# A gated recurrence, latent attention and FFN on one core: the first product behind each norm multiplies scaled inputs, and root and shift enter behind it

## The reference

```python
def rms_norm_2(x, gain=None):
    y = xf * lax.rsqrt(jnp.mean(xf * xf, axis=-1, keepdims=True) + EPS)
...
    mod = (c @ w_ada + b_ada)[:, None, :]
    sh_m, sc_m, g_m, sh_f, sc_f, g_f = jnp.split(mod, 6, axis=-1)
    h = rms_norm_2(x) * (1 + sc_m) + sh_m
    proj = h @ w_in
    x_lru, q_down, kv_down, k_rope, gate_a, gate_b = jnp.split(proj, IN_SPLIT_POINTS, axis=-1)
    y_a = rg_lru(causal_depthwise_conv(x_lru, conv_w, conv_b), ...)
    y_b = mla(q_down, kv_down, k_rope, cos, sin, q_norm_g, kv_norm_g, w_uq, w_ukv)
    y = jax.nn.sigmoid(gate_a) * y_a + jax.nn.sigmoid(gate_b) * y_b
    x = x + g_m * (y @ w_out)
    h = rms_norm_2(x) * (1 + sc_f) + sh_f
    gate, up = jnp.split(h @ w_ffn_in, 2, axis=-1)
    x = x + g_f * ((jax.nn.silu(gate) * up) @ w_ffn_out)
```

## Time and profile before

| | us |
|---|---|
| median of 3 runs | 1828.05 (1827.4 to 1828.36) |
| the profiled execution | 1825.89 |
| its span, first to last instruction | 1824.1 |
| PE busy | 1751.8 (96%) |
| DVE busy | 956.1 (52%) |
| ACT busy | 723.8 (40%) |
| POOL busy | 688.3 (38%) |

### The profile page before, as it was taken

One profiled execution on the slowest core, in us unless ns is written; L12 is line 12 of the kernel. 1 busy time (PEld: TensorE's weight loads), 2 busy tenths in 40 slices (PEclk: granted clock), 3 DMA queues, 4 the chain that ended last, 5 costly groups with the idle time before them and its releaser, 6 DMA issues. The chain is left out here.

```text
span 1824.1 us, 23408 instructions
## 1 busy us (share of the span) xinstructions
PE 1751.8 (96%) x8349; PEld 1416.4 (78%) x8349; DVE 956.1 (52%) x1746; ACT 723.8 (40%) x1244; POOL 688.3 (38%) x303
## 2 busy tenths in 40 slices
PE   7999999988999999999999999999999999999997
PEld 6777777777888766788888887888766788888886
DVE  5999688584679577633343322579665311101112
ACT  5433655523375553322222222466553333222221
POOL 3424111236430334555445554440212454444442
PEclk9999999999999999999999999999999999999998
DMA  6234010053332224455555542233211232232211
GB/s 246 81 104 139 24 32 28 24 196 128 104 104 93 81 81 140 136 194 189 194 187 185 187 148 81 87 110 104 93 35 35 69 108 100 81 115 93 93 58 47
DMA packets 56634, 197.67 MB, mean 108 GB/s; under 512 B 6993, under 2 KB 8017, under 8 KB 56530
## 3 DMA queue, kind: packets, MB, share of 16 engines
q1 hardware_dynamic: 55666, 194.15, 31.6%
q10 hardware_dynamic: 864, 2.11, 0.3%
HBM read 194.14 MB, written 2.10 MB: 108 GB/s over the span
## 5 line engine op out<-in xcount | busy, mean ns | idle before, releaser
L491 POOL TENSOR_TENSOR WL<-RAW,WH 128x1024 fp32r<-128x1024 f32 x234 | 592.5, 2537 | 900.6 <-ACT WH L580 561.8
L1743 PE MATMUL bank<-HH,WH 128*128 128x512 f32 x1120 | 437.0, 390 | 7.8 <-POOLq L496 5.9
L1745 PE MATMUL bank<-HH,WL 128*128 128x512 f32 x1120 | 435.9, 389 | 0.0
L1744 PE MATMUL bank<-HL,WH 128*128 128x512 f32 x1120 | 435.8, 389 | 0.0
L580 ACT ACTIVATE WH<-RAW 128x1024 fp32r<-128x1024 f32 x259 | 270.6, 1051 | 243.8 <-PE bank L1745 218.1
L1743 PEld LDWEIGHTS bank<-HH,WH 128*128 128x128 f32 x1120 | 210.2, 188 | 53.3 <-issue 10.2
L1745 PEld LDWEIGHTS bank<-HH,WL 128*128 128x128 f32 x1120 | 210.2, 188 | 44.0
L1744 PEld LDWEIGHTS bank<-HL,WH 128*128 128x128 f32 x1120 | 210.2, 188 | 43.4
L1676 DVE TENSOR_TENSOR HF<-SILU,bank 128x512 f32<-128x512 f32 x44 | 30.3, 688 | 314.3 <-PE bank L1745 311.3
L1743 PE MATMUL bank<-HDH,WH 128*128 128x512 f32 x352 | 137.1, 389 | 0.0
L1745 PE MATMUL bank<-HDH,WL 128*128 128x512 f32 x352 | 136.9, 389 | 0.0
(11 more groups left out here) (363 smaller groups left out, 2839.6 us busy)
## 6 DMA issues: line engine op xcount, KB each, us to landing
RAW<-in_stream SPq DMA_DIRECT2D x363, 512.0 KB, 3.3
out_t<-YA SPq DMA_DIRECT2D x8, 256.0 KB, 2.2
X<-in_xt ACTq DMA_DIRECT2D x3, 512.0 KB, 11.3
RAW<-in_stream SPq DMA_DIRECT2D x2, 256.0 KB, 4.0
X<-in_xt ACTq DMA_DIRECT2D x2, 256.0 KB, 6.4
ACC<-in_pos SPq DMA_DIRECT2D x1, 256.0 KB
gains<-in_gains SPq DMA_DIRECT2D x1, 224.0 KB
CS<-in_cs SPq DMA_DIRECT2D x1, 128.0 KB
```

Of the source, the lines that this page charges most:

```text
L491: nc.gpsimd.tensor_tensor(lo(k)[:], raw(k)[:], hi(k)[:].bitcast(F32), ALU.subtract).then_inc(sem["passed"], mark("passed", *k))
L1743: nc.tensor.matmul(out, A[0], B[0], start=first, stop=False)
L1744: nc.tensor.matmul(out, A[0], B[1], start=False, stop=False)
L1745: return nc.tensor.matmul(out, A[1], B[0], start=False, stop=last)
```

## The change

The first product behind each norm (`kvq`; `fg` and `fu` tile 0) multiplies u = X(1 + scale), split into `plain_hi` on ACT and `plain_lo` on DVE: in `YH`, `YL` at m0, in `HH`, `HL` elsewhere. The root multiplies its result at the eviction. The shift's part of the product is a sum over raw weight rows times shift (`shift_times`, DVE, in `SHA`, made beside `o1`, `o2` and `fo`), which PE adds up over the partitions (`shift_sum`, `shift_columns`); it enters at the eviction too. PE takes the square sum behind `kvq` slot 0 (behind chunk 5 of `fg`), root and shift product behind slot 1 (behind chunk 3 of `fu`). POOL adds all eight squares, the warm matmuls are gone, and h is made as before, for the products that follow. Sixteen `ada` slots instead of eight are summed in the attention, eight instead of sixteen beside `o1`; the scale block of the mixer is turned in the attention.

```diff
-        order += [ada.pop(0) for _ in range((2, 3, 3, 3, 3, 2, 0, 0)[n])]
+        order += [ada.pop(0) for _ in range((2, 2, 2, 2, 0, 0, 0, 0)[n])]
...
-                order += [ada.pop(0) for _ in range((0, 1, 2, 2, 2, 1, 0, 0)[n])]
+                order += [ada.pop(0) for _ in range((1, 2, 2, 2, 1, 0, 0, 0)[n])]
...
-                    if ada:
+                    if ada and f:
...
-ATT_ADA = tuple(range(4, 76, 9))
+ATT_ADA = tuple(range(4, 84, 5))
...
-    return key[:2] == ("ada", 0) and key[2] // 8 in (0, MLA_CB)
+    return key[:2] == ("ada", 0) and key[2] // 8 in (0, 1, MLA_CB)
...
+def shift_product(key):
+    return key[0] == "kvq" or (key[0] in ("fg", "fu") and key[2] == 0)
...
+                        if shift_product(k):
+                            pool.wait_ge(sem["shift_mul"], value("shift_mul", *k))
...
-                for k in range(1, KD - 1):
+                for k in range(1, KD - (tag == "fin")):
...
+            def plain_hi(tag, k):
+                layer, cb = int(tag[1]), 1 if tag[0] == "m" else 4
+                act.wait_ge(sem["x_new"], value("x_new", tag, k))
+                act.wait_ge(step, value("scale", layer, cb))
+                nc.scalar.activation(plain(tag)[0][:, k, :], X[:, k, :], ACT.Identity,
+                                     scale=scale_of(tag)[:, k:k + 1]).then_inc(
+                    sem["u_hi"], mark("u_hi", tag, k))
...
+                    if tag == "m1":
+                        act.wait_ge(*last_use(("kvq", 1, k // 2)))
+                    elif tag[0] == "f" and k < KD - 1:
+                        act.wait_ge(sem["u_used"], value("u_used", tag, k))
+                    elif tag[0] == "f":
+                        act.wait_ge(*last_use(("fu", int(tag[1]), 0)))
...
+                    if tag[0] == "m" and k in (2, 4, 6):
+                        split_through(("kvq", int(tag[1]), k // 2))
...
-                act.wait_ge(sem["x_new"], value("x_new", "m0", n))
+                plain_hi("m0", n)
...
-                split_through(("kvq", L, 0), 0)
+                split_through(("kvq", L, 3), 0)
...
-                for tt in range(NT):
-                    evict(KVR[:, tt, :], "kvq", L, tt)
+                evict(SPREAD[:, 0:448], "shift", L)
...
+                    if L or n >= 5:
+                        for k in range(KD) if (L, n) == (0, 5) else (n,):
+                            if k <= n:
+                                plain_hi(f"f{L}", k)
...
+                split_through(("fg", L, 0))
...
+                evict(SPREAD[:], "rb", f"f{L}")
...
-                        evict(SILU[:, f % 2, :], "fg", L, f, func=ACT.Silu)
+                        if f:
+                            evict(SILU[:, f % 2, :], "fg", L, f, func=ACT.Silu)
+                        else:
+                            act.wait_ge(sem["scaled"], value("scaled", "fg", L))
+                            nc.scalar.activation(SILU[:, 0, :], NTMP[:, 0, :], ACT.Silu, bias=SHF[:, 0:1]).then_inc(
+                                sem["read_act"], mark("read_act", "fg", L, 0))
...
+                            if tag == "m1":
+                                plain_hi(tag, n)
...
+                        note[("scale", layer, cb)] = count["step"]
+            def plain_lo(tag, k):
+                dve.wait_ge(sem["u_hi"], value("u_hi", tag, k))
+                hi_, lo_ = plain(tag)
+                V.scalar_tensor_tensor(out=lo_[:, k, :], in0=X[:, k, :], scalar=scale_of(tag)[:, k:k + 1],
+                                       in1=hi_[:, k, :].bitcast(F32), op0=ALU.mult, op1=ALU.subtract).then_inc(
+                    sem["u_lo"], mark("u_lo", tag, k))
+            def shift_times(slot, shift, parts, dst):
+                dve.wait_ge(landed[ring(slot)], loads(slot))
+                for i, (k, col) in enumerate(parts):
+                    n = dst.shape[1]
+                    src = raw(slot)[:, col:col + n]
+                    if k == 0:
+                        ins = V.tensor_scalar(dst, src, shift[:, 0:1], None, ALU.mult)
+                    else:
+                        ins = V.scalar_tensor_tensor(out=dst, in0=src, scalar=shift[:, k:k + 1], in1=dst,
+                                                     op0=ALU.mult, op1=ALU.add)
+                    if i < len(parts) - 1:
+                        ins.then_inc(step, 1)
+                        dve.wait_ge(step, own())
+                ins.then_inc(sem["shift_mul"], mark("shift_mul", *slot))
+                dve.wait_ge(sem["shift_mul"], value("shift_mul", *slot))
+            def shift_rows(layer, s):
+                shift_times(("kvq", layer, s), mod[:, layer, 0:KD], [(2 * s + c, 512 * c) for c in range(2)],
+                            SHA[:, 0:448])
+            def shift_tile(layer, i):
+                shift_times((("fg", "fu")[i], layer, 0), mod[:, layer, 3 * KD:4 * KD],
+                            [(k, P * k) for k in range(KD)], SHA[:, i * P:(i + 1) * P])
...
-                mods(("o1", n)) if n < KD - 1 else None
-            ada_through(("xl", 0, 0))
-            mods(("o1", KD - 1))
+                mods(("o1", n))
+                if n:
+                    plain_lo("m0", n - 1)
+                if 3 <= n < KD - 1:
+                    shift_rows(0, n - 3)
+            plain_lo("m0", KD - 1)
...
-                dve.wait_ge(sem["read_act"], value("read_act", "kvq", L, NT - 1))
+                dve.wait_ge(sem["read_act"], value("read_act", "shift", L))
+                for t in range(NT):
+                    dve.wait_ge(sem["full"], value("full", "kvq", L, t))
+                    V.scalar_tensor_tensor(out=KVR[:, t, :], in0=bank_of("kvq", L, t)[:, 0:448],
+                                           scalar=stat[:, 1, t:t + 1], in1=SPREAD[:, 0:448],
+                                           op0=ALU.mult, op1=ALU.add).then_inc(
+                        sem["read_dve"], mark("read_dve", "kvq", L, t))
+                dve.wait_ge(sem["read_dve"], value("read_dve", "kvq", L, NT - 1))
...
+                    if n in (3, 4):
+                        shift_tile(L, n - 3)
+                    if L == 0 and n == 5:
+                        for k in range(n):
+                            plain_lo(f"f{L}", k)
+                    elif n and (L or n > 5):
+                        plain_lo(f"f{L}", n - 1)
+                plain_lo(f"f{L}", KD - 1)
...
+                        if f == 0:
+                            dve.wait_ge(sem["full"], value("full", "shift_f", L))
+                            b = bank_of("shift_f", L)
+                            V.tensor_copy(SHF[:], b[:, 0:2]).then_inc(sem["read_dve"], mark("read_dve", "shift_f", L))
+                            dve.wait_ge(sem["read_dve"], value("read_dve", "shift_f", L))
+                            dve.wait_ge(sem["read_act"], value("read_act", "rb", f"f{L}"))
+                            for i, kind in enumerate(("fg", "fu")):
+                                dve.wait_ge(sem["full"], value("full", kind, L, 0))
+                                V.tensor_tensor(NTMP[:, i, :], bank_of(kind, L, 0)[:], SPREAD[:],
+                                                ALU.mult).then_inc(sem["scaled"], mark("scaled", kind, L))
...
-                        dve.wait_ge(sem["full"], value("full", "fu", L, f))
-                        b = bank_of("fu", L, f)
-                        V.tensor_tensor(HF[:, f % 2, :], SILU[:, f % 2, :], b[:], ALU.mult).then_inc(
-                            sem["hid"], mark("hid", L, f))
+                        if f == 0:
+                            dve.wait_ge(sem["scaled"], value("scaled", "fu", L))
+                            V.scalar_tensor_tensor(out=HF[:, 0, :], in0=NTMP[:, 1, :], scalar=SHF[:, 1:2],
+                                                   in1=SILU[:, 0, :], op0=ALU.add, op1=ALU.mult).then_inc(
+                                sem["hid"], mark("hid", L, 0))
+                        else:
+                            dve.wait_ge(sem["full"], value("full", "fu", L, f))
+                            b = bank_of("fu", L, f)
+                            V.tensor_tensor(HF[:, f % 2, :], SILU[:, f % 2, :], b[:], ALU.mult).then_inc(
+                                sem["hid"], mark("hid", L, f))
...
+                        if half and L + 1 < LAYERS:
+                            if n:
+                                plain_lo(next_norm(L), n - 1)
+                            if n == KD - 1:
+                                plain_lo(next_norm(L), n)
+                            if 3 <= n < KD - 1:
+                                shift_rows(L + 1, n - 3)
...
-                pe.wait_ge(sem[adder], value(adder, tag, KD - 2))
+                pe.wait_ge(sem[adder], value(adder, tag, KD - 1 if newest is None else KD - 2))
...
-                warm(tag, 0, 7)
+            def root_rows(tag):
...
-                warm(tag, 1, 6)
...
+            def shift_sum(layer):
+                b = claim("shift", layer)
```

(23 more changed lines are left out.)

84 lines of the change are left out of this document (55 added, 29 removed).

## The result

The changed kernel takes 1845.84 us (median of four runs, 1843.0 to 1848.88) against 1828.2 of the kernel before beside it: ratio 1.0093, 95% interval 1.0073 to 1.0112. It is slower, by 17.6 us and not by the 8 of the forecast. The profiled execution took 1845.64 us, 19.75 more than the one before.

A forecast was written before the change was run, and what follows sets the result against it. TensorE, busy 1751.8 of 1824.1 us, was taken as the bound, with DVE-POOL blocking second. Against the profiled 1825.89: +1.4 - 5.1 + 1.4 + 2.5 - 4.2 - 4.4 = 8.4 slower, 1834.3, median 1836; own range 1830 to 1841, wide 1811 to 1846.

The forecast's parts named there:

- clock term: Half-clock falls after new PE stalls, charged for two at 2.2 us each: 4.4 us slower, bounds 0 and 10.8.
- The attention: Eight more slots scaled on ACT and added on POOL make PE wait: loss 4.2 us, bounds 1.5 and 6.
- Attention output and first mixer: Output stage through first mixer: square sum stalls 3.7 us, second XCL feeds PE at 480.5 against 481.96, gain 1.4.
- The unblocked T + 48.2 of the mixer: Second layer's mixer: second XCL ready at T + 48.2, T the sum's place, without DVE-POOL blocking; gain 5.0 us.
- First FFN: First FFN norm: late scale block stalls the square sum 4.2 us, third hidden tile starts late; loss 5.1 us.
- Second mixer: Second layer's mixer: second XCL ready at T + 51.8 against T + 53.2, T the sum's place; gain 1.4 us.
- Second FFN: Second FFN norm: scale ready early, sum waits about 0.1 us, third tile starts at 27.5; gain 2.5 us.
- two longest only: Choice to charge a clock fall only at the two longest of four new stalls: 2 x 2.2 = 4.4 us.
- All four stalls that I had listed: New PE stalls above 2.8 us: 3.7, 4.2, 6.7 at the third hidden tile, 3.1 at lg0.
- The rule: DVE-POOL port lock: by it HL, YL and the latents block beside POOL, giving the sum of 8.4 us slower.
- the covers hold: Rival: DVE-POOL blocking is rare, no stall long enough for the clock; 10.7 us faster, 1817; chance 0.34.
- a fall at every long stall: Rival: each of the four long stalls drops the clock; 14.8 us slower, 1843; chance 0.08.

The follow-up runs named there:

- e6: Changed kernel with one DVE step per shift product instead of two or eight, most of the shift's part left out of four products: 1832.83 us, ratio 1.0029.
- e1: Changed kernel with matmuls of no use put on TensorE ahead of nine waits: 1836.05 us, ratio 1.0044.
- e11: Changed kernel with one step for each shift product and matmuls of no use ahead of the waits: 1829.26 us, ratio 1.0005.
- e2: Kernel before with only the new plan of w_ada slots up to the attention output, no norm changed: 1831.52 us, ratio 1.0023.
- e4: Changed kernel with the first FFN's scaled inputs using the mixer's long-ready scale block, made chunk by chunk: 1844.27 us, ratio 1.0092.
- e9: Kernel before with only the second layer's two norms changed, plus matmuls of no use ahead of waits there and around the attention: 1824.76 us, ratio 0.9988.
- e7: Kernel before without its 52 warm matmuls at the four norms, nothing else changed: 1836.22 us, ratio 1.0048.

## Why the prediction was wrong

The direction was right, and the mechanism that I named, blocking between DVE and POOL together with the clock, is what the trace shows. The size was half of it: 8 us against 17.6. The wide range ended at 1846 and takes the result in by 0.2 us, which is luck; the forecast's own ended at 1841.

Two steps of the sum failed. The shift steps beside the FFN's output tiles had no term at all, and the clock was charged 4.4 us where 16.2 more of lost work came. They overlap: e6 is 13 us better without the steps, e1 9.8 with fills, e11 16.6 with both. Without its clock term the sum said 4.0 slower, and e1's profiled execution, whose lost work is that of the kernel before, was 6.5 slower. That this is near is partly luck: in it attention and first FFN lost 9.9 and 9.4 where 4.2 and 5.1 had been taken, and the output stage with the first mixer gained 7.1 where 1.4 had been taken. By part:

- **The attention** (taken as 4.2 slower, measured 9.3). The waits were sized well: PE's idle time grew by 4.1. What failed is that I gave the attention no fall of the clock; there were two, with 4.55 us of lost work. e2 shows the whole loss with no norm changed.
- **Attention output and first mixer** (taken as 1.4 faster, measured 3.7 for the two stages). The last tile ended 5.6 sooner in its stage's time, 5.0 had been taken, and the square sum waited 0.96 instead of 3.7. DVE's last residual began at 435.43, 2.5 us behind the last tile's end (432.95) and not some 5; the two shift steps ahead of it had taken 4.44 us, not 1.2. The turn-taking that I had followed step by step was too strict, with steps that were too short. TensorE's own terms were right: the shift product took 0.92 us against 0.8, in the FFN 0.51 against 0.5. The unblocked T + 48.2 of the mixer is not the sum of the terms shown (23.8 + 2.6 + 20.4 = 46.8); it enters only the rival. The waits at xl0 and the recurrence, taken as "near 2" and 3.1, came as 1.41 and 3.28; the second, though, ended with POOL's split and not with XCL.
- **First FFN** (taken as 5.1, with the two falls charged 9.5; measured 14.7, with 5.5 of lost work). The third hidden tile's wait came as 6.74 against 6.7. The square sum's came as 7.0 against 4.2, and its main cause was another: not the late scale block with its six chunks and five lows (e4: 1.5 of it), but the shift steps. **This is the first step that failed.** The prediction charged two shift steps near 0.6 each in the mixer (the 448-column step has a mean of 1.92) and had no term at all for the sixteen steps of the two FFN tiles, though the change adds them. One 128-column step took 0.35 us where POOL left it alone, a tile of eight 5.9 to 9.9 with POOL beside it. Without them the wait is 1.44 (e6), and e6 puts 13 us on all of them together, with the falls that follow.
- **Second mixer** (1.4, measured 1.3). Right, and the first mixer would have been level with it but for a fall: 176.5 with falls at 439 and 484, 174.8 in e6 with one at 482 alone, 174.5 in e1 with none. A fall at the recurrence costs next to nothing, since PE must wait for POOL behind it: 174.6 in the second layer of the changed kernel and of e1. The fall at the square sum costs near 2.
- **Second FFN** (2.5 faster, measured 1.3 slower). The third tile began 28.3 us behind the sum's old place against the 27.5 taken and the 30.0 before: 1.7 gained. A fall at 1487 took 3.0. Without it, e1 and e9 show 410.9: the gain is there.
- **The clock** (4.4 taken, bound 10.8). **This is the second step that failed.** There were ten falls before the last norm, where I had charged two; filling the waits gives 9.8 us by the medians, so my upper bound was near, and the value, "two longest only", was the wrong choice. I had reasoned from one idle stretch of 2.50 us with no fall at 412 that short waits are safe. At 439 it fell after 0.96. All four stalls that I had listed were followed by a fall (439, 484, 764, 794), with 8.7 us of lost work in place of 10.8; the other six had no term. The kernel before without its warm matmuls (e7, 8.8 us slower) shows what they are worth there. I had named them as gone and put no price on that.
- **The rule** of the Trainium skill (SBUF — State Buffer, SBUF: two separate sides) is an exclusive lock, for a whole instruction, between a DVE instruction with two SBUF inputs and a GpSimd one that reads SBUF. The trace agrees: HL took 0.75 alone and 2.11 to 2.54 beside a split. Its row before had been no evidence, since POOL had never run beside it; the rival "the covers hold" was to be decided there, and fell.
- **The other rule** of the Trainium skill (TensorE: Matmul & The Clock Gate, Part 1) is that the gate follows how busy the engine has lately been. The trace agrees in that every fall ahead of the last norm stands behind a wait of 0.96 us or more. Its rival, a fall at every long stall, 1843, with chance 0.08, was the nearest to the result, in part by luck: it had four falls and not ten, and no shift steps.

What stays open: why the same wait is followed by a fall in one execution and not in another. There are four places (near 56, 116, 250 and 298) where it came in the profiled executions of some kernels alone. In the runs of the kernel before the time follows the mean granted clock, from 1823.68 us at 0.995 to 1833.10 at 0.987; the four runs of the changed kernel all show 0.982 or 0.983, and what spreads them from 1843 to 1849 is not shown. And blocking itself was not taken away while the work stayed: e6 leaves the steps out, it doesn't unblock them, so that the same steps without POOL beside them would cost little is argued from their durations.

## What to carry to other kernels

Work that is put beside a full stage must be counted instruction by instruction, at the duration that it has beside POOL's work (here 0.35 us alone, 0.89 in the mean), and its own followers (here the scale block and the squares) moved by it. Where a change takes away matmuls that compute nothing, or turns one long gap into several short waits, the clock has to be priced as a term of its own: ask of every wait what TensorE does in it, and try to fill it. A fall ahead of a later wait for another engine is cheap, as at the recurrence. Work moved behind a norm's wait is only covered if everything that hangs on it, down to the weights of the third hidden tile, is ready in time as well.

## What the runs showed that was not expected

- Leaving out 52 matmuls without a use made the kernel before 8.8 us slower (1836.22 against 1827.4); adding some ahead of nine waits made the changed kernel 9.8 us faster.
- The granted clock fell to 0.50 after 0.96 us of waiting with a sum of eight one-column matmuls behind it (439), and after a wait of 1.26 in the attention (224), and did not after 2.50 at 412 in the kernel before.
- A step of `shift_times` takes 0.35 us for 128 columns at its shortest and up to 2.83 in the whole run; the 448-column step has a mean of 1.92.
- The second mixer took 174.6 us with a fall at the recurrence (changed kernel) and without one (e1).
